# A four-mixer decoder layer in fp32: inverse products on four array quarters, and an opening by token blocks

## What is computed

```
def reference(x, meta, norm1_g, w_in, ...):
    x = concat(pads, meta, x)
    h = _rms(x, norm1_g) * valid
    z = h @ w_in
    y_sb  = stick_breaking_attention(aq, ak, av)
    y_ret = retention(bq, bk, bv) * silu(bg)
    y_rw  = rwkv7_mix(*rwkv7_project(c_in, ...))
    y_sw  = sliding_window_attention(dq, dk, dv, ...)
    x += (sum_i sigmoid(gate_i) * (y_i @ P_i)) @ w_o
    x += squared_relu_mlp(_rms(x, norm2_g), w_up, w_down)

def rwkv7_mix(...):
    def step(S, inp):
        S = S * w_t - outer(S @ kk_t, b_t) + outer(v_t, k_t)
        return S, S @ r_t
```

## Time and profile before

| | |
|---|---|
| timed executions, median (lowest, highest) | 1309.74 us (1306.81, 1312.76) |
| profiled execution | 1307.6 us |
| its span from first to last instruction | 1305.8 us |
| PE busy | 1230.2 us, 94% of the span |
| ScalarE, GpSimd, VectorE busy | 487.2, 467.0, 464.8 us |
| share of the chain that ended last | PE 77%, DVE 11%, ACT 6% |
| moved by DMA | 110.17 MB, mean 84 GB/s |

### The profile page before, as it was taken

One profiled execution on the slowest core, in us unless ns is written; L12 is line 12 of the kernel. 1 busy time (PEld: TensorE's weight loads), 2 busy tenths in 40 slices (PEclk: granted clock), 3 DMA queues, 4 the chain that ended last, 5 costly groups with the idle time before them and its releaser, 6 DMA issues.

```text
span 1305.8 us, 21002 instructions
## 1 busy us (share of the span) xinstructions
PE 1230.2 (94%) x9042; PEld 1014.9 (78%) x9042; DVE 464.8 (36%) x834; ACT 487.2 (37%) x784; POOL 467.0 (36%) x287
## 2 busy tenths in 40 slices
PE   5999999989999999999899999889899999999998
PEld 4998877877789768767577777668788888788886
DVE  3599322323232262444263485362422100122000
ACT  6456312212222243677544635331543311233210
POOL 2443425143423223423331432233144544244541
PEclk9999989999999999999999999999899999999999
DMA  6222322113221113110511221142132333122330
GB/s 230 82 66 87 116 74 88 47 58 106 74 72 38 50 52 113 61 36 33 213 66 57 83 81 49 49 145 81 49 97 93 111 102 97 61 89 95 116 126 33
DMA packets 33340, 110.17 MB, mean 84 GB/s; under 512 B 4048, under 2 KB 6064, under 8 KB 32608
## 3 DMA queue, kind: packets, MB, share of 16 engines
q1 hardware_dynamic: 25952, 92.44, 21.5%
q10 hardware_dynamic: 6784, 16.26, 3.4%
q0 software_dynamic: 512, 0.13, 0.1%
HBM read 99.42 MB, written 9.04 MB: 83 GB/s over the span
## 4 chain that ended last, share of the span: by engine, by line
PE 77%; DVE 11%; ACT 6%; issue 2%; POOL 2%; DMA 2%; ACTq 0%; DVEq 0%; SPq 0%; POOLq 0%
PE pst L1623 17%; PE pst L1624 15%; PE pst L1625 15%; PE pst L1778 4%; PE pst L1777 4%; PE pst L1776 4%; PE pst L2076 2%; PE pst L2067 2%; DMA sw_v<-wait_sw_v 1%; ACT w_hi L784 1%; PE pst L1815 1%; PE pst L1802 1%; DVE merged L1309 1%; PE pst L2093 1%; PE pst L2051 1%
## 5 line engine op out<-in xcount | busy, mean ns | idle before, releaser
L667 POOL TENSOR_TENSOR w_lo<-raw,w_hi 128x1024 fp32r<-128x1024 f32 x164 | 401.2, 2452 | 714.9 <-ACT w_hi L784 703.3
L1623 PE MATMUL pst<-h_hi,w_hi 128*128 128x512 f32 (+1 forms) x960 | 357.7, 373 | 4.1 <-DVE x L1328 2.6
L1624 PE MATMUL pst<-h_lo,w_hi 128*128 128x512 f32 (+1 forms) x960 | 346.2, 361 | 0.0
L1625 PE MATMUL pst<-h_hi,w_lo 128*128 128x512 f32 (+1 forms) x960 | 346.0, 360 | 0.0
L784 ACT ACTIVATE w_hi<-raw 128x1024 fp32r<-128x1024 f32 x164 | 171.1, 1050 | 147.1 <-PE pst L1778 114.3
L1623 PEld LDWEIGHTS pst<-h_hi,w_hi 128*128 128x128 f32 x960 | 182.8, 190 | 40.6 <-issue 5.7
L1624 PEld LDWEIGHTS pst<-h_lo,w_hi 128*128 128x128 f32 x960 | 182.9, 190 | 27.4 <-issue 2.2
L1625 PEld LDWEIGHTS pst<-h_hi,w_lo 128*128 128x128 f32 x960 | 182.5, 190 | 27.7
L1623 PE MATMUL pst<-w_hi,h_hi 128*128 128x256 f32 (+3 forms) x328 | 94.2, 288 | 6.8 <-DVE h_lo L1495 3.7
L1778 PE MATMUL pst<-w_hi,u_lo 128*128 128x512 f32 x256 | 99.6, 389 | 0.0
L1777 PE MATMUL pst<-w_lo,u_hi 128*128 128x512 f32 x256 | 99.6, 389 | 0.0
(11 more groups left out here) (320 smaller groups left out, 1751.0 us busy)
## 6 DMA issues: line engine op xcount, KB each, us to landing
raw<-in_weights SPq DMA_DIRECT2D x164, 512.0 KB, 3.4
xt<-in_x SPq DMA_DIRECT2D x4, 512.0 KB, 5.4
wait_gate<-stage ACTq DMA_DIRECT2D x8, 256.0 KB, 2.0
gate_t<-wait_gate ACTq DMA_DIRECT2D x1, 2048.0 KB, 8.9
x<-in_x ACTq DMA_DIRECT2D x1, 2048.0 KB, 8.6
out<-x SPq DMA_DIRECT2D x8, 256.0 KB, 3.3
cst<-in_consts SPq DMA_DIRECT2D x1, 1524.0 KB, 10.4
wait_ret_v<-stage ACTq DMA_DIRECT2D x8, 128.0 KB, 1.9
```

Of the source, the lines that this page charges most:

```text
L667: nc.gpsimd.tensor_tensor(w_lo[:, u % W_SLOTS, :], raw[:, u % RAW_SLOTS, :], w_hi[:, u % W_SLOTS, :].bitcast(F32), ALU.subtract).then_inc( ...
L1623: M(out, lh, rh, start=(first and i == 0), stop=False)
L1624: M(out, lh, rl, start=False, stop=False)
L1625: last = M(out, ll, rh, start=False, stop=(final and i == len(terms) - 1))
```

## The change

It has two parts.

**Opening by token blocks.** The norm's gain is loaded as a row (`gain_row`, a new input) and spread over 128 partitions by two outer products with a row of ones, into PSUM banks 6 and 7. VectorE's scaling now multiplies by the inverse norm and by this gain in one operation. PE transposes a whole token block at a time (four feature tiles to a bank), in the order block 0, meta, block 1, then 2 and 3; `h_hi` and `h_lo` are made from each bank with a plain copy and a subtraction. Columns 0 to 271 need blocks 0, meta and 1 only: job 1's first half stands before the transposes of blocks 2 and 3, and job 2's first half, job 1's second and job 2's second follow. SyncE's transfers are put in the order in which they are needed.

**Four quarters.** In C1, U, F and WZ, heads of odd parity now give their results to the other half of the output partitions and to a bank of their own, so that the four matmuls of a head pair (two heads, two chunks) lie on four different quarters. C1 and U lie side by side in a bank pair. The copies and additions behind them come in three parts: even heads on 128 rows, odd heads of each chunk on 64 rows, read from the other half. The second copy of F goes to VectorE and the second copy of WZ to ScalarE. Some semaphores are merged.

```diff
+        def turned(b):
+            if b == 0:
+                return [(slice(0, MB), slice(0, MB))]
+            return [(slice(CH * i, CH * i + CH), slice(CH - CH * i, P - CH * i)) for i in range(2)]
+        def by_parity(b, g):
+            h0, every = 4 * g, slice(0, rw_blocks[b][0])
+            return [(every, every, slice(h0, h0 + 4, 2), 4 + 2 * g)] + \
+                   [(to, at_, slice(h0 + 1, h0 + 4, 2), 5 + 2 * g) for to, at_ in turned(b)]
+        def out_rows_of(b, h):
+            return [at_ if h % 2 else to for to, at_ in turned(b)]
...
+            token_block(0)
+            sp.dma_start(cst[:, 0:P], consts[:, 0:P]).then_inc(turn_in, 16)
+            sp.wait_ge(zeros_ready, 2)
+            sp.dma_start(xm[MB - N_META:MB, :], meta).then_inc(x_in, 16)
+            token_block(1)
+            weight_unit(0)
+            token_block(2)
+            token_block(3)
+            sp.dma_start(par[:], params).then_inc(const_in, 16)
+            for u in range(1, RAW_SLOTS):
+                weight_unit(u)
+            sp.dma_start(cst[:, P:NCONST], consts[:, P:NCONST]).then_inc(table_in, 16)
+            sp.dma_start(lor[:], lora).then_inc(table_in, 16)
...
-                        A(C1[0:n, 4 * g:4 * g + 4, 0:m], four(pst[0:n, 4 + 2 * g, 0:256])[:, :, 0:m], ACT.Copy)\
-                            .then_inc(c1_copied[g], 1)
+                        for to, at_, hs, bank in by_parity(b, g):
+                            last = A(C1[to, hs, 0:m], two(pst[at_, bank, 0:128])[:, :, 0:m], ACT.Copy)
+                        last.then_inc(c1_copied[g], 1)
...
+            def token_norm(b):
+                dve.wait_ge(rs_ready, TOKEN_ORDER.index(b) + 1)
+                V.scalar_tensor_tensor(out=halves(src), in0=halves(src), scalar=rs0[0:r, b:b + 1], in1=pst[0:r, 6:8, :],
+                                       op0=ALU.mult, op1=ALU.mult).then_inc(hn_ready, 1)
...
-                            V.tensor_tensor(XX[0:n, hs, 0:m], XX[0:n, hs, 0:m],
-                                            four(pst[0:n, 5 + 2 * g, 0:256])[:, :, 0:m], ALU.add).then_inc(added, 1)
+                            for to, at_, hp, bank in by_parity(b, g):
+                                last = V.tensor_tensor(XX[to, hp, 0:m], XX[to, hp, 0:m],
+                                                       two(pst[at_, bank, 256:384])[:, :, 0:m], ALU.add)
+                            last.then_inc(added, 1)
...
+            for i in range(2):
+                last = M(pst[:, 6 + i, :], ones_row[:], gain_row[:, T * i:T * i + T], start=True, stop=True)
+            last.then_inc(ht_done, 1)
...
+            for b in (0, NB, 1):
+                token_turn(b)
+            feature_job(PHASE_C[0], ALL, 0, 2)
+            token_turn(2)
+            token_turn(3)
+            feature_job(PHASE_C[1], ALL, 0, 2)
+            feature_job(PHASE_C[0], ALL, 1, 2)
+            feature_job(PHASE_C[1], ALL, 1, 2)
...
+            def places(b, g):
+                return [(rows, out_rows_of(b, h)[ci], h) for t in (2 * g, 2 * g + 1)
+                        for ci, (rows, _, _) in enumerate(chunks_of(b)) for h in (2 * t, 2 * t + 1)]
...
-                        for h in range(4 * g, 4 * g + 4):
-                            o = CH * (h % 4)
-                            for rows, _, _ in chunks:
-                                last = M(pst[rows, 4 + 2 * g, o:o + m], MM[rows, step % 2, h, 0:m],
-                                         TT[rows, h, 0:m], start=True, stop=True)
+                        for rows, out_rows, h in places(b, g):
+                            o = CH * (h % 4 // 2)
+                            last = M(pst[out_rows, 4 + 2 * g + h % 2, o:o + m], MM[rows, step % 2, h, 0:m],
+                                     TT[rows, h, 0:m], start=True, stop=True)
```

More of the change, by code:

```diff
@@ L216, with build @@
 SBUF_BASE, SBUF_END = 16512, 229344
-def build(nc, x, meta, weights, lora, consts, params, out):
+def build(nc, x, meta, weights, lora, consts, params, gain, out):
     with ExitStack() as ctx:
@@ L491, in halves, with h_bank, h_parts @@
             return row.rearrange("p (a b) -> p a b", a=2)
+        TOKEN_ORDER = [0, NB, 1, 2, 3]
+        def h_bank(b, half):
+            return [2, 4, 4, 6][b] + half
+        def h_parts(b):
+            if b == NB:
+                return [(pst[:, 1, 0:KD * MB].rearrange("p (k c) -> p k c", k=KD), (slice(0, KD), slice(0, MB)), 3)]
+            cols, n = slice(MB + P * b, MB + P * b + P), [1, 4, 6, 8][b]
+            return [(pst[:, h_bank(b, i), :].rearrange("p (k c) -> p k c", k=4), (slice(4 * i, 4 * i + 4), cols), n + i)
+                    for i in range(2)]
         def job_slot(n):
@@ L659, in _ @@
         def _(pool):
+            nc.gpsimd.memset(ones_row[:], 1.0).then_inc(zeros_ready, 1)
             nc.gpsimd.memset(xm[:], 0.0).then_inc(zeros_ready, 1)
@@ L792, in _, with token_scale @@
             A = nc.scalar.activation
+            act.dma_start(gain_row[:], gain).then_inc(turn_in, 16)
             nc.scalar.preload_act_table_set("natural_log_exp_and_others")
-            for b in list(range(NB - 1)) + [NB, NB - 1]:
+            def token_scale(b):
                 r, src = (P, xt[:, b, :]) if b < NB else (MB, xm[:])
@@ L2082, in _ @@
                     pe.wait_ge(x_ready[g], level0[b] + levels_of[b])
-                    for h in range(4 * g, 4 * g + 4):
-                        for rows, _, _ in chunks:
-                            last = M(pst[rows, 4 + 2 * g, HD * (h % 4):HD * (h % 4) + HD], AM[rows, h, 0, 0:m],
-                                     VT[rows, HD * h:HD * h + HD], start=True, stop=True)
+                    for rows, out_rows, h in places(b, g):
+                        o = HD * (h % 4 // 2)
+                        last = M(pst[out_rows, 4 + 2 * g + h % 2, o:o + HD], AM[rows, h, 0, 0:m],
+                                 VT[rows, HD * h:HD * h + HD], start=True, stop=True)
                     last.then_inc(f_done, 1)
```

186 lines of the change are left out of this document (105 added, 81 removed).

## The result

| | before | changed |
|---|---|---|
| timed executions, median (lowest, highest) | 1310.03 us (1306.81, 1312.76), 4 runs | 1290.44 us (1289.54, 1291.94), 4 runs |
| profiled execution; its span | 1307.6; 1305.8 | 1290.54; 1288.7 |
| ratio, 95% interval | | 0.9853 [0.9828, 0.9877] |

That two parts hide in this sum, one larger and one smaller than forecast, is what the rest is about.

What follows compares the result with a forecast made beforehand. PE was taken to bound the kernel. RWKV (-18.7 + 0.3 + 0.9 = -17.5 us) and the opening (-5.5) made -23.0, taken from the median of 1309.7: 1286.7 us, range 1280 to 1297.

Steps and rivals of the forecast that it cites:

- The pitch: C1 and U groups: four quarters start records every 14.7 ns instead of 29, so 32 records take 0.47 us instead of 0.94.
- Rival (c): Four-quarter groups: a bank serves one row half at a time, pitch stays 29 ns; 1307.7 us, no change; chance 0.07.
- (b): Four-quarter groups: quarters sharing banks overlap only partly, pitch near 22 ns, 9.3 us of gain lost; 1296 us; chance 0.10.
- I take the same for ACT and for 64 rows: Copies behind the groups: three small ones take 0.7 us on ACT too, as on DVE, 0.3 more than one.
- 0.75 us to spare: RWKV levels: the dense piece between C1 and U groups hides the longer copies with this much room.
- rival (d): RWKV levels: small copies outlast the pieces; PE waits from 0.34 us each, at 0.6 us each 1345 us; chance 0.04.
- the 0.3 charged: RWKV level whose piece is a dv job: too little room for ACT's copies before U, 0.3 us added.
- 0.47 x 40: RWKV levels, blocks 1 to 4: 0.47 us saved in each of 40 C1 and U groups, 18.7 us less.
- F and WZ, +0.9: Behind each block's last level: PE work saved turns into waits for uncovered copies, 0.9 us more over all blocks.
- The opening, -5.5: Opening: first product at about 15.7 instead of 24.07, 5.5 us less at the end; bounds -0.5 and -7.
- Rival (a): Opening: clock rises late or the start is later than 15.7, only -0.5 to -2.5; 1290.7 us; chance 0.16.
- 3.8 sufficed before: Opening: 3.8 us of products halved the pitch before, so 5.4 us without a gap should do so ahead of the transposes.

Runs made afterwards that it cites:

- e4: Changed kernel, with the even heads' copies of F and WZ on ACT and the odd heads' on DVE, for both halves; 1288.93 us, ratio 0.9834.
- e2: Kernel before with the opening by token blocks alone; 1303.35 us, ratio 0.9942.
- e8: Same kernel as e4, measured again beside the changed kernel on another chip; 1289.59 us, ratio 0.9842.
- e5: Changed kernel once more, unedited; 1291.94 us, ratio 0.9870 to the kernel before.
- e9: Changed kernel a third time, unedited; 1293.67 us, ratio 0.9864 to the kernel before.
- e7: Changed kernel, with all five token blocks transposed ahead of the first product and the opening's two jobs uncut; 1295.02 us, ratio 0.9879.
- e1: Kernel before with the four quarters alone, opening as before; 1299.47 us, ratio 0.9914.

## Why the prediction was right, and where it was not

**The pitch (rivals b and c).** Right. 0.47 us a group was forecast and 0.453 came. With both row halves writing one bank, 32 records take 0.69 us with their tail, as a full overlap of four quarters would have it. The rule of the Trainium skill that I had set against it (TensorEngine Tiling (Array Packing), Restrictions and Gotchas: different row tiles cannot access the same bank simultaneously) doesn't hold here, where they write disjoint output halves: by it the groups would have stayed at 1.15. Rival (c), no change, falls with it, and (b).

**"I take the same for ACT and for 64 rows".** This step failed in size for ACT. Three operations of 128 columns take DVE 0.89 us and ACT 0.84 to 0.85, where I had 0.7; ACT's lie 0.29 apart, as long as each lasts, while the 0.21 of the earlier trace rows were read between two different operations of DVE. In the covered levels it costs nothing: "0.75 us to spare" was 0.36, and rival (d), whose threshold was x = 0.34, was nearer than its chance of 0.04 suggests: x is 0.28. In the dv level it cost more than the 0.3 charged. Before and changed:

```profile
366.15 1.15 PE L2067 MATMUL pst<-rw_t,rw_m 64*64 64x64 f32 x32
368.79 1.15 PE L2076 MATMUL pst<-rw_x,rw_c 64*64 64x64 f32 x32
```
```profile
347.23 0.69 PE L2163 MATMUL pst<-rw_t,rw_m 64*64 64x64 f32 x32
348.81 1.70 ACT L1203 ACTIVATE rw_c<-pst 128x128 f32<-128x128 f32 x6
349.69 0.46 PE L2171 MATMUL pst<-rw_x,rw_c 64*64 64x64 f32 x16 [0.21 <-ACT rw_c L1203]
350.56 0.46 PE L2171 MATMUL pst<-rw_x,rw_c 64*64 64x64 f32 x16 [0.41 <-ACT rw_c L1203]
```

The U group is torn in two. From the start of C1 to the first piece behind U it is 3.72 us before and now, so these two groups bring nothing instead of 0.9.

**"0.47 x 40".** The number of groups was off. The four C1 groups of level 1 don't have their two halves together, in the kernel before either, since the second waits for POOL's mask. Block 1, before and changed:

```profile
197.75 0.68 PE L2067 MATMUL pst<-rw_t,rw_m 64*64 64x64 f32 x16
198.62 0.68 PE L2067 MATMUL pst<-rw_t,rw_m 64*64 64x64 f32 x16 [0.19 <-POOL rw_m L744]
```
```profile
189.69 0.46 PE L2163 MATMUL pst<-rw_t,rw_m 64*64 64x64 f32 x16
190.56 0.46 PE L2163 MATMUL pst<-rw_t,rw_m 64*64 64x64 f32 x16 [0.41 <-POOL rw_m L789]
```

The second half starts 0.87 us after the first in both: the first half's gain turns into a longer wait, and the earlier trace rows had such waits already, in its 5.1 us of idle time until POOL (4.3 of them are one wait ahead of block 2's first group, unchanged now). At the full clock such a group brings 0.22 us, the four 0.9 in all instead of 1.8. Together: 34 x 0.453 + 0.9 + 0 for the dv level's two is 16.3 against the 18.4 forecast.

**F and WZ, +0.9.** The mechanism was right (the PE work saved turns into waits for copies) and the size was off: +2.2 at equal clock (+2.8 in the first profile, with 0.6 from a low clock in block 0). F to WZ takes 1.79 in block 1 (1.6 forecast) and WZ to the next products 2.08 (1.85), both from the small copies' length, WZ's three being 1.29 us long and 0.44 apart where I had 1.0 and 0.34. e4 shows that sharing them between the engines would have made it a gain of 1.3.

**The clock in the RWKV stage.** No term, and no rival, held it: about +2.5 on average, as far as the profiles and the runs' mean clocks show it, with a cause that stays open. The sum took the stage's clock to be that of before.

**The opening, -5.5.** The chain came out nearly as worked out (gain products from 4.74, first product 15.37 for 15.7, second job 31.4 for 31.9), and the 0.8 us kept back for handshakes were hardly used: 6.7 in the first profile, 6.9 in e2's, and 5.7 (e8's) at the least. Rival (a) fell, but more narrowly than the first profile shows. "3.8 sufficed before" was read from one execution: in the three profiles of before the pitch halves 4.1, 3.5 and 5.0 us after the first product. In the seven with the new opening the 24 products last 4.9 to 5.6 us. In four of them the pitch halves within these products; in e5, e9 and e8 all or nearly all of them run at the low pitch, and in e8 the first three transposes too:

```profile
21.20 2.21 PE L1750 MATMUL pst<-cst,xt 128*128 128x128 f32 x16
```

That the rise came ahead of the transposes or just into them every time is partly luck. Once it had come, they ran at the high pitch and did not lower it. The Trainium skill says (TensorE: Matmul & The Clock Gate, Part 4: PE-mode transpose) that transposes don't engage the full clock. The kernel before agrees, with 10 us of them at the low pitch; e7's last 16, at 3.68 us, stand behind 3.51 us of idle time and say less. That they would hold a raised clock down is not in the page, and the changed kernel shows that 16 of them don't.

**The sum.** -16.3 + 2.2 + 2.5 for the clock is -11.6 for the quarters, and e1 measured -11.3; -6.7 for the opening, -7.6 in e2. That is -18.3 to -18.9, against -18.7 between the means of all executions and -19.6 between the medians of the first comparison. The forecast of -23.0 had missed by what the quarters give back: 2.1 in the levels, 1.3 at F and WZ, 2.5 through the clock, with 1.2 more from the opening on the other side. The mechanism of both parts held; that the clock's 2.5 us stayed within the range is luck, since no term or rival had them.

## What to carry to other kernels

Where matmuls are made to run four abreast, price the copies behind them as strictly as the matmuls: small copies on one engine lie end to end, cost the same on 64 rows as on 128, and are free only where a piece of other work stands between; where none does, share them between two engines at once. When adding up groups, count only those whose two halves run through, and look in the row's idle time for the ones that wait for something else. And profile the kernel before more than once before a loss of a few us in an unchanged stage is explained: here two such profiles differed by 6.7 us.

## What the runs showed of the hardware

- ACT's short copies out of PSUM don't overlap: 0.29 us apart at 271 to 274 ns each, whether on 128 rows in place or on 64 rows read from the other half of the partitions. DVE's additions of the same shapes cost 272 and 286 ns, 0.30 apart.
- Two row halves writing one PSUM bank in the same group, to different output halves, cost the array nothing: 32 records take 0.69 us on four quarters and 1.15 on two, for the C1 and the U line (640 records each).
- A profiled execution of the same kernel spends 34 to 51 us (before) or 41 to 54 us (changed) at a granted clock of 0.50 (1.2 GHz), and its span follows by several us. Over 28 executions of before the mean clock went from 0.980 to 0.986 and the time from 1315.9 to 1305.5 us.
- Sixteen fp32 transposes between products ran at the high pitch (1.91 us; 3.68 behind idle time) and left it there. In e8 the pitch halved only behind the third of them (2.21 us).
- Low-clock stretches come back at the same places of the program in one execution and not in the next: near 494 us in two of three profiles of before, near 474 in all three of the changed kernel.
